# Fifth input-projection group of a hybrid decoder step: first four slabs plain fp32, last four as three fp32r products

## The reference

```python
h = _rmsnorm(x, p['norm_mix_w'])
a_v, a_g, b_u, c_z, c_xbc, c_dt = jnp.split(h @ p['w_in'], IN_SPLITS, axis=-1)
...
_, _, h_re, h_im = lax.associative_scan(_complex_affine_combine, (a_re, a_im, bu_re, bu_im), axis=1)
y = (jnp.einsum('blgp,ghp->blgh', h_re, c_re.astype(f32))
     - jnp.einsum('blgp,ghp->blgh', h_im, c_im.astype(f32)))
```

## Time and profile before

| | us |
|---|---|
| median of 3 runs (lowest, highest) | 1803.45 (1802.83, 1803.63) |
| the profiled execution, its own time | 1805.04 |
| its span, first to last instruction | 1803.3 |
| TensorE busy in the span | 1784.9 |
| VectorE, ScalarE, GpSimd busy | 1139.3, 739.2, 258.9 |

### The profile page before, as it was taken

How to read it: one execution, slowest core, us unless ns; L and a number is a source line. 1 busy time by engine, 2 the same in 40 slices (tenths; PEclk the granted TensorE clock), 3 DMA queues, 4 the chain that set the end, 5 groups by cost and what they waited for, 6 DMA issues and landing times.

```text
span 1803.3 us, 32857 instructions
## 1 busy us (share of the span) xinstructions
PE 1784.9 (99%) x12594; PEld 1640.2 (91%) x12594; DVE 1139.3 (63%) x1976; ACT 739.2 (41%) x1111; POOL 258.9 (14%) x273
## 2 busy tenths in 40 slices
PE   8999999999999999999999999999999999999998
PEld 7877898777779999866999999999999999999998
DVE  6999888888775564443456556665655566546444
ACT  3100575444453343342245344444433345444444
POOL 1024200133421310000132000000000000003200
PEclk9999999999999999999999999999999999999999
DMA  8333544556667585487555555555555556554552
GB/s 255 106 117 106 198 140 138 176 182 208 196 209 240 164 303 164 153 327 265 154 164 164 164 163 163 163 163 164 164 166 165 165 148 185 166 163 160 167 163 99
DMA packets 158390, 316.49 MB, mean 176 GB/s; under 512 B 16986, under 2 KB 39531, under 8 KB 153492
## 3 DMA queue, kind: packets, MB, share of 16 engines
q1 hardware_dynamic: 153525, 307.73, 54.5%
q10 hardware_dynamic: 4776, 7.56, 1.4%
HBM read 300.78 MB, written 14.89 MB: 175 GB/s over the span
## 4 chain that ended last, share of the span: by engine, by line
PE 93%; DVE 4%; DMA 2%; ACT 1%; issue 0%; ACTq 0%; SPq 0%; DVEq 0%
PE bank L909 22%; PE bank L911 21%; PE bank L910 21%; PE bank L872 20%; PE bank L1467 2%; PE bank L1479 1%; DVE xc L2638 1%; DMA kv<-in_cache_mem_v 1%; DMA xtok<-in_x_prompt 1%; PE bank L1489 1%; PE bank L1278 0%; DMA raw<-in_w_out 0%; DVE raw_lo L2665 0%; PE bank L1097 0%; PE bank L958 0%; PE bank L1312 0%
## 5 line engine op out<-in xcount | busy, mean ns | idle before, releaser
L909 PE MATMUL bank<-hhi,whi 128*128 128x288 f32 x2128 | 631.9, 297 | 0.9 <-DVE wlo L2918 0.9
L910 PE MATMUL bank<-hlo,whi 128*128 128x288 f32 x2128 | 628.5, 295 | 0.0
L911 PE MATMUL bank<-hhi,wlo 128*128 128x288 f32 x2128 | 626.3, 294 | 0.0
L2918 DVE TENSOR_TENSOR wlo<-raw,whi 128x1024 fp32r<-128x1024 f32 (+1 forms) x270 | 329.7, 1222 | 377.7 <-ACT whi L1950 377.1
L1950 ACT ACTIVATE whi<-raw 128x1024 fp32r<-128x1024 f32 (+1 forms) x270 | 283.2, 1049 | 509.8 <-PE bank L911 501.9
L911 PEld LDWEIGHTS bank<-hhi,wlo 128*128 128x128 f32 x2128 | 401.6, 189 | 0.0
L909 PEld LDWEIGHTS bank<-hhi,whi 128*128 128x128 f32 x2128 | 399.3, 188 | 2.3 <-DVE wlo L2918 1.9
L910 PEld LDWEIGHTS bank<-hlo,whi 128*128 128x128 f32 x2128 | 400.2, 188 | 0.1
L872 PE MATMUL bank<-hT,raw 128*128 128x288 f32 x640 | 160.1, 409 | 0.0
L872 PEld LDWEIGHTS bank<-hT,raw 128*128 128x128 f32 x640 | 120.0, 190 | 35.0 <-issue 3.1
L1877 ACT ACTIVATE khi<-raw 128x1024 fp32r<-128x1024 f32 x66 | 69.9, 1059 | 109.5 <-PE bank L872 106.4
(11 more groups left out here) (551 smaller groups left out, 2744.4 us busy)
## 6 DMA issues: line engine op xcount, KB each, us to landing
raw<-in_ffn_w_down SPq DMA_DIRECT2D x86, 512.0 KB, 3.8
raw<-in_ffn_w_gate SPq DMA_DIRECT2D x80, 512.0 KB, 3.7
raw<-in_ffn_w_up SPq DMA_DIRECT2D x80, 512.0 KB, 3.7
raw<-in_w_in SPq DMA_DIRECT2D x64, 512.0 KB, 3.7
raw<-in_xa_wk SPq DMA_DIRECT2D x32, 512.0 KB, 3.9
raw<-in_xa_wv SPq DMA_DIRECT2D x32, 512.0 KB, 4.2
raw<-in_w_out SPq DMA_DIRECT2D x32, 512.0 KB, 3.8
raw<-in_xa_wq SPq DMA_DIRECT2D x32, 512.0 KB, 4.0
```

The lines of the kernel that those rows point to most:

```text
L909: pe.matmul(out, lhsT=wh[:, wo:wo + P], rhs=xh, start=first, stop=False)
L910: pe.matmul(out, lhsT=wh[:, wo:wo + P], rhs=xl, start=False, stop=False)
L911: return pe.matmul(out, lhsT=wl[:, wo:wo + P], rhs=xh, start=False, stop=last)
L2918: tt(wlo[:, s % 2, wsl], raw[:, s % 4, wsl], whi[:, s % 2, wsl].bitcast(F32), ALU.subtract)\
```

## The change

`SPLIT_AT` goes from 40 to 36: the last four slabs of the fifth group (36 to 39) are split slabs, the first four stay plain. Since these four multiply tiles 8 to 15 of the input, ScalarE rounds tiles 8 to 15 in place after group 3's slabs, and tiles 0 to 7 after slabs 32 to 35; TensorE waits for the roundings in that order (`XHI_AT`). The four subtractions that come earlier, and the two for slabs 40 and 41, are written into S5's turns 14 and 15 on VectorE. The last `s5_out` moves from after slab 39 to after slab 40 (`S5_OUT`); the others stay. The blocks `x_high` and `in_split` on ScalarE only move up in the file.

```diff
-        SPLIT_AT = 40
+        SPLIT_AT = 36
+        XHI_AT = [k - 8 if k >= 8 else k + 8 for k in range(16)]
+        S5_OUT = (22, 25, 27, 30, 32, 35, 37, 40)
...
-                                    pe.wait_ge(*at("x_hi", k + 1))
+                                    pe.wait_ge(*at("x_hi", XHI_AT[k] + 1))
...
-                    if x == S5_IN[pair] + 5:
+                    if x == S5_OUT[pair]:
...
-                    wait_used_A(sc_, SPLIT_AT - 8 + k // 2)
+                    wait_used_A(sc_, (24 if k >= 8 else 32) + k // 2)
...
+            x_high(range(8, KT))
...
-            x_high(range(12))
-            in_split(SPLIT_AT)
-            x_high(range(12, 14))
+            in_split(36)
+            x_high(range(4))
+            in_split(37)
+            x_high(range(4, 8))
+            in_split(38)
+            in_split(39)
+            in_split(40)
             in_evac(4)
-            in_split(SPLIT_AT + 1)
-            x_high(range(14, KT))
+            in_split(41)
...
             for j in range(SJ):
+                if j == 15:
+                    in_split(38)
                 v.wait_ge(*at("s5_in", j // 2 + 1))
...
+                if j == 14:
+                    in_split(36)
                 v.wait_ge(*at("s5_turned", 2 * j + 2))
...
+                if j == 15:
+                    in_split(39)
                 me.sync()
...
+                if j == 14:
+                    in_split(37)
+                if j == 15:
+                    in_split(40)
                 if j >= 1:
                     s5_turn_back(j - 1)
...
+            in_split(41)
             s5_turn_back(SJ - 1)
...
-            in_split(SPLIT_AT)
-            in_split(SPLIT_AT + 1)
```

More of the change, by code:

```diff
@@ L1768, in _, with x_high, in_split @@
             in_evac(3)
+            def x_high(tiles):
+                for k in tiles:
+                    wait_used_A(sc_, (24 if k >= 8 else 32) + k // 2)
+                    sc_.wait_ge(*at("x_lo", k + 1))
+                    a(xhi[:, k, :], hT[:, k, :], ACT.Copy).then_inc(S("x_hi"), 1)
+            def in_split(x):
+                wait_raw(sc_, x // 4, x % 4)
+                if x >= SPLIT_AT + 2:
+                    wait_used_A(sc_, x - 2)
+                if x == 48:
+                    sc_.wait_ge(*at("s5_prod", 2 * SJ))
+                    sc_.wait_ge(*at("s5_turned", 2 * SJ))
+                a(ihi_slot(x), raw[:, x % 4, :], ACT.Copy).then_inc(S("kw_hi"), 1)
+            x_high(range(8, KT))
             def first_tap(dst, dst_s, src, src_s, w, b, name):
@@ L1790, in gelu @@
                     a(uT[:, t, :], uT[:, t, :], ACT.Gelu_apprx_tanh).then_inc(S("s5_gelu"), 1)
-            def x_high(tiles):
-                for k in tiles:
-                    wait_used_A(sc_, SPLIT_AT - 8 + k // 2)
[L1796 to L1807, removed]
             def mem_square(t):
@@ L1877, in k_split @@
                 a(khi[:, y % 2, :], raw[:, y % 4, :], ACT.Copy).then_inc(S("kw_hi" if y < NKV else "w_hi"), 1)
-            for x in range(SPLIT_AT, NA):
+            for x in range(40, NA):
                 if x == NA - 1:
@@ L1882, in _ @@
                     k_split(0)
-                elif x > SPLIT_AT:
+                elif x > 40:
                     in_split(x + 1)
@@ L2543, in last_state, with in_split @@
                     me.step(v.tensor_copy(fin[:, i, j:j + 1], hri[:, j % 2, i, NP - 1:NP]))
+            def in_split(x):
+                v.wait_ge(*at("kw_hi", x - SPLIT_AT + 1))
+                tt(raw_lo[:, x % 4, :], raw[:, x % 4, :], ihi_slot(x).bitcast(F32), ALU.subtract)\
+                    .then_inc(S("kw_lo"), 1)
             for j in range(SJ):
+                if j == 15:
+                    in_split(38)
                 v.wait_ge(*at("s5_in", j // 2 + 1))
```

## The result

The changed kernel takes **1808.1 us** (median of 9 runs, 1807.05 to 1810.88); the kernel before, on the same chip, 1804.68 us (9 runs, 1802.83 to 1806.85). The ratio is 1.002, with a 95% interval of 1.0011 to 1.003: slower by 3.4 us. The forecast was +4.0 us, 1807.4.

The account below looks back on a forecast made before the run. TensorE, busy 99% of the span, was taken as the bound. Pauses 3.65 + 1.05 + 1.8 less 3.1 for products gave +3.4, the clock +0.6: +4.0 on 1803.45, so 1807.4 us, range 1804.5 to 1809.0.

Parts of the forecast that it names:

- first pause: TensorE waits in front of slab 36 for VectorE's late subtraction, starting at 194.25 instead of 190.58: 3.65 us lost.
- second pause: TensorE waits in front of slab 37 for its subtraction, at full clock until 198.55: 1.05 us lost.
- third pause: Last S5 output, in front of slab 41, waits for VectorE's last turn back, 212.5 to 214.3: 1.8 us lost.
- four slabs: Slabs 36 to 39 on TensorE, split instead of plain, go from 15.92 to 12.86 us: 3.1 us less.
- sum at full clock: Start of slab 41: the three pauses less the savings on products, +3.4 us, before any clock loss.
- clock, net: Clock falls after the 3.65 us pause, losing 1.7 us; the wait before slab 37 swallows 1.05: +0.6 us.
- (B): Rival: the pauses come in slabs 36 to 41, but the clock holds: +3.4 us, 1806.9; chance 0.23.
- (D): Rival: VectorE and POOL disturb each other less, little but the pause before slab 36 stays: from +1.1, 1805.0; chance 0.14.
- (C): Rival: the waits are longer, by POOL's order or by `glu_w`: 1808.5 us; chance 0.14.
- (E): Rival: VectorE's standstill is no wait for TensorE, slab 36's subtraction is in time, 3.1 us won: 1800.4; chance 0.05.
- (F): Rival: the split slabs cost as much as plain ones; with the pauses 1810 us; chance 0.02.
- upper bound: POOL's second product goes first (1.25 us) and `glu_w` loads later (another 1): some +5.5 us, 1809.0.

Follow-up runs that it names:

- e7: The changed kernel once more, unchanged, for a second profile: 1807.23 us, ratio 1.0016.
- e2: The changed kernel plus seven small products of ones on TensorE ahead of its wait for slab 36: 1808.18 us, ratio 1.0018.
- e4: Changed kernel, pair 5's output after slab 34, slabs 36 and 37 rounded and subtracted earlier, last two ways back before subtractions 40 and 41: 1802.37 us, 0.9983.
- e1: The changed kernel with pair 5's S5 output products issued after slab 34 instead of 35: 1803.88 us, ratio 0.9996.
- e3: The changed kernel with VectorE's last two ways back moved ahead of the subtractions of slabs 40 and 41: 1807.04 us, ratio 1.001.
- e6: The kernel before, all slabs plain, with pair 5's S5 output products after slab 34 instead of 35: 1803.55 us, ratio 0.9994.
- e8: The kernel before once more, unchanged, for a second profile: 1804.93 us, ratio 1.0001.

## Why the prediction was right

The mechanism and the sum held: the stage lost 3.97 us in one profile and 4.00 in the other, where the working had +4.0. By the medians the loss is 3.4 us, and 2.5 in e7, with intervals some 3 us wide; the mean of all 19 runs of the changed kernel lies 3.6 us above the mean of the 32 of before that e7 was compared with. The forecast was laid on the median of three runs, 1803.45; the many runs of before have 1804.7 to 1804.8. From there +4.0 would have given 1808.7, so part of the closeness of 1807.4 to 1808.1 is luck: a base too low and a loss a little too high. By its steps, at full clock as e2 shows them:

| term | predicted | measured | where |
|---|---|---|---|
| first pause | 3.65 | 3.47 | e2: 190.66 to 194.13, the seven products within it |
| second pause | 1.05 | 0.81 | e2 |
| third pause | 1.8 | 1.80 | e2 |
| four slabs | -3.1 | -2.7 | e2: 13.25 us for slabs 36 to 39, 15.92 before |
| sum at full clock | +3.4 | +3.48 | e2 against before |
| clock, net | +0.6 | +0.49 | changed against e2 |

*Mis-sized.* The four slabs: I took 3.26 and three times 3.20, 12.86 us. In e2 they take 3.42, 3.36, 3.27 and 3.20 (from each one's first product to the next start, less the wait). The two dearer ones lie beside the pauses, slab 36 between two and slab 37 behind one; the rows that I read had no pause beside them. In e4 slab 38 too, with the pause of 0.32 us behind it, takes 3.42. The three pauses together were 0.4 us too long in the forecast, and that the two errors cancel is luck.

*The first pause.* VectorE resumed at 190.67, where about 190.6 was forecast. The subtraction slipped in beside POOL as that sum had done: predicted 192.9 to 194.1, measured 192.67 to 194.06, with POOL's second product stretched to 2.27 us. TensorE followed 0.10 us later, not 0.15. e1 shows the cause by removing it: no standstill, and 0.86 us are left of the pause.

*The second pause.* It doesn't stand in the profile of the changed kernel, because the slow clock swallowed it, as forecast; e2 brings it out.

*The third pause.* Predicted from 212.5 to 214.3, measured 1.79 us to 214.87, 0.6 us later on the axis, as the clock's net loss has it. e3 shows the cause: with the way back first, it is gone and 1.86 us with it.

*The clock.* Predicted 1.7 us of loss after the pause, measured 1.7. The Trainium skill, "TensorE: Matmul & The Clock Gate", section "HAM oscillation — how this bites in real kernels", says that gaps bring the array back to half clock; all three pauses of 3.45 us agree (0.60 and 0.50 at 195 and 196 in the changed kernel, 0.50 at 196 in e3 and at 194 in e7), and e2's idle time of 1.64 us, behind seven small products, does not bring it about.

*The rivals.* (B) fell with the clock at 0.50, (D) because all three pauses are there, the second in e2. (C) asked for longer waits: after slab 42 no new one appears in the list of waits, so `glu_w`'s later load cost TensorE nothing. (E) needed VectorE to resume before 188; it resumed at 190.67. What (E) would have brought is real in the main: e4 makes it true by moving the work, and wins 2.74 us against before and 2.16 against e6, where (E) had 3.1. (F) fell with the length of the slabs.

*The upper bound.* Its terms do not give its sum: 1.25 and 1 on top of +4.0 are +6.25, not +5.5. Nothing hung on it, since neither term came: the subtraction went ahead of POOL's second product, and no wait for `glu_w` shows.

*Open.* Whether the changed kernel meets the fall near 870 less often than the one before isn't settled by one profile without and one with it. It could be why the medians show less than +4.0; the scatter of the medians could be as well.

## What to carry to other kernels

A cheaper form of a product moves work to the engine that prepares its operands. Before counting the gain, walk that engine's queue: if the new preparation stands behind a wait for the bounding engine itself, the bounding engine waits for its own past, and a few microseconds go in pauses. Here the products that VectorE waited for and the new subtractions could both be moved, and neither alone was enough: each left VectorE late elsewhere, and the third pause stayed. The two together, with the ways back put first, won the time. Whether one of them with the ways back put first would have won most of it was not run; as an estimate from e1 and e3, e1's 0.49 us above before less e3's 1.86 would be some 1.4 us below it.

## What the runs showed of the hardware

The granted clock is not the same from run to run at the same place. A wait of 1.7 to 1.9 us for a load, somewhere between 838 and 848 us, stands in all ten profiles; in nine the clock stayed at 1.00 after it, in e8 it fell to 0.53; the 43 small transposes were followed by 0.50 in seven of ten profiles. Each fall loses about 1.7 us, nearly half the difference that this study was about, so two profiled spans are not compared before their falls are counted.

VectorE's two-input instructions and POOL's products wait for each other here rather than share. The subtraction at 211.41 took 2.32 us where it takes 1.22 alone: it began 0.05 us after a product of POOL, which ended at 212.65, and ended 1.08 us after that. In the other direction POOL's product at 192.93 took 2.27 us where it takes 1.27, with a subtraction under way until 194.06; it ended 1.14 us after it, and the sum that began at 193.98 took 1.50 us in its turn.
